# One decoder block on one core: the input loads in smaller pieces, and the first projection in rows of three passes

## What is computed

```
h = rms_norm(x, norm1_gain)
proj = h @ w_in                      # 1024 -> 3600 columns: gq|gk, gv, gr, g_low (16), mq, mk, mv
log_a = log_sigmoid(g_low @ w_gate_up + b_gate) / 16
o_gla = gated linear attention of (gq, gk, gv, log_a), normed, times silu(gr)
o_moba = causal attention of (rotary(mq, positions), rotary(mk, positions), mv), normed
x = x + concat(o_gla, o_moba) @ w_out
x = x + (silu(rms(x) @ w_ffn_gate) * (rms(x) @ w_ffn_up)) @ w_ffn_down
return rms_norm(x, final_norm_gain)
```

## Time and profile before

| | value |
|---|---|
| runs, us | 314.45, 314.82, 314.95 |
| profiled execution, us | 314.64 |
| its span, first to last instruction, us | 312.6 |
| TensorE matmul busy | 302.2 us, 97% |
| TensorE weight load busy | 252.8 us, 81% |
| VectorE busy | 179.5 us, 57% |
| ScalarE busy | 154.4 us, 49% |
| GpSimd busy | 22.7 us, 7% |
| moved by DMA | 54.45 MB, mean 174 GB/s |

### The profile page before, as it was taken

One profiled execution on the slowest core, in us unless ns is written; L12 is line 12 of the kernel. 1 busy time (PEld: TensorE's weight loads), 2 busy tenths in 40 slices (PEclk: granted clock), 3 DMA queues, 4 the chain that ended last, 5 costly groups with the idle time before them and its releaser, 6 DMA issues.

```text
span 312.6 us, 3884 instructions
## 1 busy us (share of the span) xinstructions
PE 302.2 (97%) x1430; PEld 252.8 (81%) x1430; DVE 179.5 (57%) x201; ACT 154.4 (49%) x188; POOL 22.7 (7%) x45
## 2 busy tenths in 40 slices
PE   5999999999999999999999999999999999999991
PEld 5787888888888888888888888888888888888881
DVE  0788979986696346646271908082635536280454
ACT  2977897569553336362433516070807152443124
POOL 7130100000202000600000000000000000000012
PEclk9999999999999999999999999999999999999998
DMA  6987386536844302928374564729090928330003
GB/s 215 364 273 258 96 311 189 212 134 247 267 146 149 134 0 78 305 89 273 132 226 179 175 228 132 270 77 325 23 360 19 317 85 275 128 134 0 0 2 135
DMA packets 36449, 54.45 MB, mean 174 GB/s; under 512 B 2834, under 2 KB 25668, under 8 KB 36436
## 3 DMA queue, kind: packets, MB, share of 16 engines
q1 hardware_dynamic: 36212, 54.05, 50.4%
q0 software_dynamic: 64, 0.03, 0.2%
q10 hardware_dynamic: 160, 0.20, 0.2%
HBM read 53.23 MB, written 1.05 MB: 174 GB/s over the span
## 4 chain that ended last, share of the span: by engine, by line
PE 94%; DMA 2%; ACT 1%; DVE 0%; POOL 0%; SPq 0%; issue 0%; POOLq 0%
PE acc L440 16%; PE acc L442 16%; PE acc L441 16%; PE aux L440 13%; PE aux L442 13%; PE aux L441 13%; PE aux L529 4%; DMA raw<-in_w_in 2%; PE aux L607 1%; PE aux L629 1%; PE aux L589 1%; PE aux L575 1%; POOL ms_f L428 0%; ACT reuse_f L994 0%; PE aux L536 0%; PE acc L503 0%
## 5 line engine op out<-in xcount | busy, mean ns | idle before, releaser
L1027 DVE TENSOR_TENSOR w_lo<-raw,w_hi 128x2048 fp32r<-128x2048 f32 x48 | 107.8, 2286 | 15.1 <-ACT w_hi L808 15.1
L808 ACT CAST w_hi<-raw 128x2048 fp32r<-128x2048 f32 x48 | 89.8, 1915 | 6.4 <-PE acc L442 4.7
L440 PE MATMUL aux<-w_hi,aT_hi 128*128 128x512 f32 (+1 forms) x180 | 70.8, 393 | 0.0
L442 PE MATMUL aux<-w_hi,aT_lo 128*128 128x512 f32 (+1 forms) x180 | 69.8, 388 | 0.0
L441 PE MATMUL aux<-w_lo,aT_hi 128*128 128x512 f32 (+1 forms) x180 | 69.6, 387 | 0.0
L440 PE MATMUL acc<-w_hi,aT_hi 128*128 128x512 f32 x134 | 54.1, 404 | 0.6 <-DVE w_lo L1043 0.6
L442 PE MATMUL acc<-w_hi,aT_lo 128*128 128x512 f32 x134 | 52.4, 391 | 0.0
L441 PE MATMUL acc<-w_lo,aT_hi 128*128 128x512 f32 x134 | 52.2, 390 | 0.0
L1250 DVE TENSOR_TENSOR pT_lo<-aux,pT_hi 128x512 fp32r<-128x512 f32 x10 | 6.9, 692 | 70.2 <-ACT pT_hi L969 70.2
L969 ACT CAST pT_hi<-aux 128x512 fp32r<-128x512 f32 x10 | 5.9, 586 | 76.4 <-PE aux L529 76.4
L442 PEld LDWEIGHTS aux<-w_hi,aT_lo 128*128 128x128 f32 x180 | 33.8, 188 | 7.0
(11 more groups left out here) (173 smaller groups left out, 242.0 us busy)
## 6 DMA issues: line engine op xcount, KB each, us to landing
raw<-in_w_in SPq DMA_DIRECT2D x24, 512.0 KB, 5.0
raw<-in_w_ffn_gate SPq DMA_DIRECT2D x22, 512.0 KB, 4.1
raw<-in_w_ffn_up SPq DMA_DIRECT2D x22, 512.0 KB, 5.4
raw<-in_w_ffn_down SPq DMA_DIRECT2D x22, 512.0 KB, 5.8
raw<-in_w_out SPq DMA_DIRECT2D x8, 512.0 KB, 4.0
x_sb<-in_x SPq DMA_DIRECT2D x2, 512.0 KB, 3.9
reuse_a<-in_final_norm_gain SPq DMA_DIRECT2D x1, 512.0 KB, 4.1
out<-reuse_e SPq DMA_DIRECT2D x2, 256.0 KB, 2.3
```

Of the source, the lines that this page charges most:

```text
L440: nc.tensor.matmul(dst, left_hi[:, k, tok], right_hi, start=first, stop=False)
L442: return nc.tensor.matmul(dst, left_lo[:, k, tok], right_hi, start=False, stop=last)
L808: nc.scalar.copy(w_hi[:, slot % RING, :], raw[:, slot % RAW, :]).then_inc(hi_ready, 1)
L1027: nc.vector.tensor_tensor(w_lo[:, slot % RING, :], raw[:, slot % RAW, :], w_hi[:, slot % RING, :].bitcast(f32), ALU.subtract).then_inc(lo_ ...
```

## The change

In words, engine by engine:

- SP: after the two tiles of x, units 0 and 1 are loaded as eight pieces of one channel chunk each (128x512, 256 KB), each with its own semaphore. Then the gate-rank columns and unit 2 as before. Units 3 and 4 wait for pieces 0 to 3 and 4 to 7 to be split.
- GpSimd: the loads of positions and frequencies are issued after L414 instead of first.
- TensorE: warm-ups are matmuls of 128x256 on a zeroed tile, 6 ahead of everything, 5 ahead of x's transposes, 1 behind them. Then eight rows: for each k the high-by-high pass for both token tiles, then high by low, then low by high, and each pass waits only for its own operands. `gate_low` and the other gains follow all eight rows, in banks 2 and 3 of `aux`. `logits` moves into the middle of unit 2, `cumulate` behind unit 3.
- ScalarE: casts pieces 1 to 7 one by one, between x's chunks.
- VectorE: zeroes the warm-up tile, casts piece 0 itself, then takes the low parts of pieces and chunks; `split(1)` is gone. Its order from `lowT` on is unchanged.

```diff
+EARLY = 2
 def fill(u):
-    return u // RAW + (1 if u % RAW else 0)
+    return u // RAW + (1 if u % RAW >= EARLY else 0)
...
+        warm = w_lo[:, RING - 1, 0:SEQ]
...
             for t in range(T):
                 sp.dma_start(x_sb[:, t, :], x[0, t * P:(t + 1) * P, :]).then_inc(x_loaded[t], 16)
+            for n in range(4 * EARLY):
+                sp.dma_start(raw[:, n // 4, (n % 4) * 512:(n % 4 + 1) * 512],
+                             w_in[0, n * P:(n + 1) * P, BLOCKS[0]:BLOCKS[0] + 512]).then_inc(first_loaded[n], 16)
...
-                if isinstance(u, int) and u == RAW:
-                    sp.wait_ge(first_lo_ready, 4)
+                if isinstance(u, int) and u < RAW + EARLY:
+                    sp.wait_ge(first_lo_ready, 4 * (u - RAW + 1))
                 else:
-                    sp.wait_ge(lo_ready, u - RAW)
+                    sp.wait_ge(lo_ready, u - RAW - EARLY + 1)
...
-            for u in range(1, RAW):
+            for u in range(EARLY, RAW):
                 rows_unit(u, w_in[0], (u % 2) * 4 * P, 4, BLOCKS[u // 2], 512)
...
+            def warm_up(n):
+                for _ in range(n):
+                    nc.tensor.matmul(acc[:, 2, 0:SEQ], warm[:, 0:P], warm, start=True, stop=True)
+
+            pe.wait_ge(warm_built, 1)
+            warm_up(6)
             pe.wait_ge(ident_built, 1)
             pe.wait_ge(norm1_loaded, 16)
...
-            warm_up(4)
+            warm_up(5)
...
-            warm_up(8)
...
+            warm_up(1)
+            def first_row(k):
+                right_hi, right_lo = weights(k // 4, 512, k % 4)
+                toks = [slice(t * P, (t + 1) * P) for t in range(T)]
+                pe.wait_ge(xT_hi_ready, k + 1)
+                pe.wait_ge(first_hi_ready, k) if k else pe.wait_ge(row0_hi_ready, 1)
+                for t in range(T):
+                    nc.tensor.matmul(acc[:, t, :], aT_hi[:, k, toks[t]], right_hi, start=k == 0, stop=False)
+                pe.wait_ge(first_lo_ready, k + 1)
+                for t in range(T):
+                    nc.tensor.matmul(acc[:, t, :], aT_hi[:, k, toks[t]], right_lo, start=False, stop=False)
+                pe.wait_ge(xT_lo_ready, k + 1)
+                for t in range(T):
+                    last = nc.tensor.matmul(acc[:, t, :], aT_lo[:, k, toks[t]], right_hi, start=False, stop=k == KC - 1)
...
-            midway = {3: [cumulate], 6: [lambda: moba_transposed(0)], 7: [lambda: moba_transposed(1)],
+            midway = {2: [logits], 6: [lambda: moba_transposed(0)], 7: [lambda: moba_transposed(1)],
...
-            after = {0: [gate_low, other_gains], 1: [logits], 4: [gla_transposed], 6: [gla_scores],
-                     7: [moba_scores], 9: [moba_outputs]}
-            for u in range(IN_UNITS):
-                if u == 0:
-                    first_unit()
-                else:
-                    in_unit(u, midway.get(u, ()))
+            after = {3: [cumulate], 4: [gla_transposed], 6: [gla_scores], 7: [moba_scores], 9: [moba_outputs]}
+            for k in range(KC):
+                first_row(k)
+            gate_low()
+            other_gains()
+            for u in range(EARLY, IN_UNITS):
+                in_unit(u, midway.get(u, ()))
...
             take_xT((0, 1))
-            split_first(0)
-            take_xT((2, 3))
-            split_first(1)
-            take_xT((4, 5, 6, 7))
+            for n in range(1, KC):
+                split_first(n)
+                if n % 2:
+                    take_xT((n + 1, n + 2) if n < KC - 1 else ())
...
-            split(1)
+            split(2)
             for t in range(T):
-                act.wait_ge(x_loaded[t], 16)
                 sum_squares(0, t)
-            split(2)
...
+            def split_first(n):
+                slot, cols = n // 4, slice((n % 4) * 512, (n % 4 + 1) * 512)
+                if n:
+                    dve.wait_ge(first_hi_ready, n)
+                else:
+                    dve.wait_ge(first_loaded[0], 16)
+                    nc.vector.tensor_copy(w_hi[:, 0, cols], raw[:, 0, cols]).then_inc(row0_hi_ready, 1)
+                    dve.wait_ge(row0_hi_ready, 1)
...
+            nc.vector.memset(warm.bitcast(f32), 0.0).then_inc(warm_built, 1)
...
-            for k in range(4):
-                take_xT((k,))
-                split_first(k)
-            take_xT((4, 5, 6, 7))
-            split(1)
+            split_first(0)
+            take_xT((0, 1))
+            for n in range(1, KC):
+                split_first(n)
+                if n % 2:
+                    take_xT((n + 1, n + 2) if n < KC - 1 else ())
             dve.wait_ge(low_in_psum, 1)
-            nc.vector.tensor_copy(lowT[0:2 * RANK, :], acc[0:2 * RANK, 2, 0:SEQ]).then_inc(lowT_ready, 1)
+            nc.vector.tensor_copy(lowT[0:2 * RANK, :], aux[0:2 * RANK, 2, 0:SEQ]).then_inc(lowT_ready, 1)
             dve.wait_ge(gains_in_psum, 2)
-            nc.vector.tensor_copy(gains[:, KC:GAIN_ROWS], acc[:, 3, 0:GAIN_ROWS - KC]).then_inc(gains_ready, 1)
+            nc.vector.tensor_copy(gains[:, KC:GAIN_ROWS], aux[:, 3, 0:GAIN_ROWS - KC]).then_inc(gains_ready, 1)
             split(2)
             split(3)
```

More of the change, by code:

```diff
@@ L191, in build_block @@
         bias_loaded = sem("bias_loaded")
-        first_loaded = [sem(f"first_loaded_{n}") for n in range(2)]
+        first_loaded = [sem(f"first_loaded_{n}") for n in range(4 * EARLY)]
+        warm_built = sem("warm_built")
+        row0_hi_ready = sem("row0_hi_ready")
         up_loaded = sem("up_loaded")
@@ L373, in then @@
                 pool.wait_ge(pool_seq, n_seq[0])
-            with nc.allow_non_contiguous_dma(reason="256 positions, one per partition and tile"):
-                pool.dma_start(pos_i[:, :], positions.rearrange("b (t p) -> p (b t)", p=P)).then_inc(pos_loaded, 16)
-            pool.dma_start(freq[:, :], inv_freq.to_broadcast([P, HALF])).then_inc(pos_loaded, 16)
             then(nc.gpsimd.memset(ident[:, :], 0.0))
@@ L415, in _ @@
                                     low_w[:, :, :, 0, :].bitcast(f32), ALU.subtract).then_inc(low_lo_ready, 1)
+            with nc.allow_non_contiguous_dma(reason="256 positions, one per partition and tile"):
+                pool.dma_start(pos_i[:, :], positions.rearrange("b (t p) -> p (b t)", p=P)).then_inc(pos_loaded, 16)
+            pool.dma_start(freq[:, :], inv_freq.to_broadcast([P, HALF])).then_inc(pos_loaded, 16)
             for t in range(T):
@@ L444, in unit_ready @@
             def unit_ready(u):
-                pe.wait_ge(hi_ready, u)
-                pe.wait_ge(lo_ready, u)
+                pe.wait_ge(hi_ready, u - EARLY + 1)
+                pe.wait_ge(lo_ready, u - EARLY + 1)
             def weights(slot, width, k, lo=0, hi=None):
@@ L457, in _ @@
                                 ident[0:KC, 0:KC]).then_inc(gains_in_psum, 1)
-            def warm_up(n):
-                for _ in range(n):
-                    nc.tensor.transpose(acc[:, 2, 0:P], ident[:, :], ident[:, :])
-            warm_up(4)
+            warm_up(5)
             for t in range(T):
@@ L472, in _ @@
                         last.then_inc(xT_in_psum, 1)
-            warm_up(8)
-            def first_unit():
-                for k in range(4):
[L479 to L485, removed]
+            warm_up(1)
[12 more added lines that the diff above has]
+                    last = nc.tensor.matmul(acc[:, t, :], aT_lo[:, k, toks[t]], right_hi, start=False, stop=k == KC - 1)
+                    if k == KC - 1 and t == 0:
+                        last.then_inc(tile0_in_psum, 1)
+                if k % 4 == 3:
+                    last.then_inc(unit_used, 1)
             def other_gains():
@@ L489, in other_gains @@
                 pe.wait_ge(rows_loaded, 48)
-                nc.tensor.transpose(acc[:, 3, 0:GAIN_ROWS - KC], other_rows[0:GAIN_ROWS - KC, :],
+                nc.tensor.transpose(aux[:, 3, 0:GAIN_ROWS - KC], other_rows[0:GAIN_ROWS - KC, :],
                                     ident[0:GAIN_ROWS - KC, 0:GAIN_ROWS - KC]).then_inc(gains_in_psum, 1)
@@ L501, in gate_low @@
                     left = w_hi[:, RING - 1, k * P:(k + 1) * P]
-                    nc.tensor.matmul(acc[:, 2, 0:SEQ], left, aT_hi[:, k, :], start=k == 0, stop=False)
-                    last = nc.tensor.matmul(acc[:, 2, 0:SEQ], left, aT_lo[:, k, :], start=False, stop=k == KC - 1)
+                    nc.tensor.matmul(aux[:, 2, 0:SEQ], left, aT_hi[:, k, :], start=k == 0, stop=False)
+                    last = nc.tensor.matmul(aux[:, 2, 0:SEQ], left, aT_lo[:, k, :], start=False, stop=k == KC - 1)
                 last.then_inc(low_in_psum, 1)
@@ L509, in in_unit @@
                 unit_ready(u)
-                if b == 1 and h == 0:
-                    pe.wait_ge(lowT_ready, 1)
-                    pe.wait_ge(gains_ready, 2)
                 if b >= 2 and h == 0:
@@ L832, in take_xT @@
                                   gains[:, NORM1_ROW + k:NORM1_ROW + k + 1]).then_inc(xT_hi_ready, 1)
[L834 to L837, removed]
```

(18 more changed lines are left out.)

13 lines of the change are left out of this document (3 added, 10 removed).

## The result

The changed kernel takes 319.05 us, the median of four runs (318.49 to 320.03), against 314.74 us before (four runs): the ratio is 1.0146, with a 95% interval of 1.0132 to 1.0160. It is 4.3 us slower. The profiled execution took 318.49 us, its span is 316.5 us; against the profiled one before (314.64) that is +3.85.

The account below looks back on a forecast made before the run. TensorE's work bounds the kernel (94% of the chain of waits). Row start -2.8 and stalls +2.9, +0.9 and +1.35 sum to +2.35 us: 314.64 + 2.3 = 316.9 us, range 315.6 to 318.6.

Parts of the forecast that it names:

- The start of the rows: Opening: first row of products starts at 7.5 us instead of 10.28, a gain of 2.8 us.
- unit 2: Behind the rows and gate product: unit 2 starts at 23.6 us, after TensorE waits for split(2).
- split(4): Ahead of unit 4: TensorE waits 0.9 us for VectorE's split(4), starting at 38.4 us against 37.45 before.
- the keys: Middle of unit 7: TensorE waits 1.35 us for the rotated keys before transposing them.
- part 2: Between gate product and unit 2: VectorE does split(2) only after two copies, so TensorE stands still about 2.9 us.
- rival (a), second case: After the stall before unit 2: half rate loses 1.5 to 2.5 us; chance 0.2, shared with late full rate at opening.
- TensorE's durations double after the stall: Behind the 2.9 us stall ahead of unit 2: a sign that would show the forecast wrong.
- the landing of the first piece: Opening: the first 256 KB weight piece lands at 6.4 us, with bounds of 5.7 and 8.1.
- the rate in the opening: Opening: TensorE reaches full rate at 7.0 us, 5.5 us after its stream starts near 1.5.
- (b): Only the stall before unit 2 opens, the later chains make up 2 us: 314.2 to 315.9 us; chance 0.09.
- (c): Opening: rows start so early that the stalls don't eat the gain, about 313.9 us; chance 0.03.
- (d): Opening: weight pieces land late or further apart, rows start at 9.0 or trickle, 318.4 us; chance 0.08.

Follow-up runs that it names:

- experiment 1: The changed kernel with VectorE doing split(2) before it waits for the gate product; 314.71 us, ratio 1.0007 to the kernel before.
- experiment 4: The changed kernel with split(9) moved behind the rotation of the keys on VectorE; 317.82 us, ratio 1.0107.
- experiment 5: The changed kernel with split(2) before the gate-product wait and split(9) behind the key rotation, 313.60 us; with split(4) also earlier on ScalarE and VectorE, 312.89 us.
- experiment 3: The changed kernel rerun unchanged, 318.90 us; and with 12 more warm-up matmuls behind the other gains, 317.59 us.
- experiment 6: Three edits, each on the changed kernel plus 22 warm-ups: position loads first, 318.57 us; no early warm-ups, 317.92; units 0 and 1 in 512 KB transfers, 317.84.

## Why the prediction was right and where it was wrong

**Right: direction, places and order.** The kernel became slower, by a wait for split(2) that the head start could not pay for, and by two more waits at the named places. The start of the rows (7.5 against 7.70), unit 2 (23.6 against 23.55), split(4) (0.9 against 0.9) and the keys (1.35 against 1.3) came out within 0.2 us. Experiments 1, 4 and 5 remove the waits one by one, with the edit that the explanation asks for.

**Wrong: the price of the stand-still.** The measured 319.05 us lie above the range of 315.6 to 318.6. The step that failed is in part 2: it priced 2.9 us of idle TensorE at 2.9 us, and the sum has nothing for the rate behind it. The loss of the full rate stood only in rival (a), second case, with a chance of 0.2 for two mechanisms together and 1.5 to 2.5 us. One of the prediction's own signs of being wrong, that TensorE's durations double after the stall, came true in substance (0.39 to 0.63 us, 0.23 to 0.43 from start to start).

Of the 2.15 us between 316.9 and 319.05, 1.6 are this loss; the other half a microsecond is the distance from the profiled execution (318.49) to the median, which the late first pieces below would explain, but no profile shows it. The size given in rival (a) was right, 1.6 us measured, and so was what it drags along (the logits late, nothing hidden). The chance was wrong: of the two profiled executions of the changed kernel one lost the rate, and the clocks of the other six runs fit a loss in each. With experiment 4, two of three profiled stand-stills of 2.7 us were followed by it, and 11 of 12 by the mean clocks. The reason given against it, that the engine is busy on both sides of the stall, carried no weight. The kernel before could not show this: its longest wait, 3.6 us, comes ahead of all work, with the engine at half rate anyway. With no row that showed the stall to be free, its cost was to be bounded from both sides. The Trainium skill (TensorE: Matmul & The Clock Gate, Why this matters for your kernels) warns of idle gaps between bursts of matmuls, and of longer ones than this. This case's trace shows the same fall behind a shorter gap, with a clock of 0.51 behind 2.70 us of waiting, though not each time.

**Right once, and mostly late: the landing of the first piece.** It was taken as 6.4 us, with 5.7 to 8.1 as bounds. The casts began at 6.48 in the first profile of the changed kernel, and from 6.72 to 7.83 in the others with the same loads. In six of those eight TensorE waited for the cast, where the forecast's main line had the operands ready first (7.1 against 7.4). Where the cast began after 7.2, the rows began at 7.9 to 8.4 (0.2 to 0.7 us later than in the first profile), the later passes waited as well, and the second row began at 9.5 to 10.1 instead of 9.09: a late piece costs 0.4 to 1.0 us. The eight runs of the changed kernel spread over 2.5 us, the ten of the kernel before beside them over 0.8; piece and rate are the two differences that the profiles show.

**Half right: the rate in the opening.** "5.5 us after the start of the stream" gave 7.0 us. In the first profile it came near 7.2 to 7.5, six us after 1.25; in the second the 16 transposes took 2.49 us and not 3.48, so it came sooner. The kernel without the early warm-ups had it by 8.4. The rule was a guess from one row, and the bounds of 7.0 and 8.6 for the start were what counted.

**Rivals.** (b) and (c) are out: both later waits opened in each kernel that kept VectorE's order. (d) is in part what the late pieces do, at 0.4 to 1.0 us of its 1.5. The transfers of 256 KB did not pay a fixed cost one after the other: their casts and rows followed without a wait. So the rule on batching (the Trainium skill, DMA: Bandwidth & Descriptors, Bandwidth) did not decide here; the pairs of 512 KB were no faster (1.0100 against 1.0085), and no run tried the 1 MiB of the rule.

## What to carry to other kernels

When a change takes work out from between two dependent steps, look at what that work was hiding. Here the 24 products of unit 1 covered a copy and a split on VectorE, and the edit that moved them should have moved split(2) too; with four such moves of order, the same early start is worth 0.6%. The length of TensorE's wait need not be its price: behind the waits of 2.2 and 2.7 us here, half rate mostly cost 1.6 us more. Filling all or half of the 2.7 us with matmuls that compute nothing kept the rate; moving one split out of the way took the wait itself.

## What the runs showed of the hardware that was not expected

- Waits of 2.70 and 2.20 us between matmuls were followed by 3 to 4 us at a granted clock of 0.50 in three of the four profiled executions that had one; waits of 1.5, 1.5, 1.1 and 1.1 us (experiments 1 and 3) were not.
- The clock fell only when the engine was at work again: 1.0 us of products at full rate came first in the changed kernel (23.55 to 24.55 us), 0.9 us in experiment 4, and 0.4 us in experiment 6.
- The same first piece, issued at the same time, was taken up between 6.48 and 7.83 us, while x landed within 0.1 us of the same time after its issue (medians 3.7 to 3.8 us). The DMA engines had moved less by then where it was late: 260 GB/s between 5 and 6 us in the execution with 6.48, 168 GB/s in the one with 7.83. Why, no run shows.
- VectorE's cast of 128x512 took 0.43 us (0.6 was assumed), less than the 0.69 us of a subtraction of that shape.
